# Moving the page gather of two of eight sequences from the second layer into the first, on one core

## What is computed

```python
# layer 0 (even): pooling and gating mixer, then a mixture of experts
y = concat([a_out, b_out]) @ w_out              # the first output projection
x = LN(alpha * x + y)
x = LN(alpha * x + moe(x))
# layer 1 (odd): RWKV-7 recurrence beside latent attention, then a mixture of experts
y = concat([y_c, y_d]) @ w_out
x = LN(alpha * x + y);  x = LN(alpha * x + moe(x))

# sample group, latent attention of layer 1: 2048 past positions = 16 pages of 128
def page_step(carry, pages):                    # scanned over page_table.T
    ck = pool_ckv[pages]                        # (8 sequences, 128 positions, 128)
    kp = pool_kpe[pages]                        # (8 sequences, 128 positions, 32)
    return online_update(carry, scores(q_lat, q_pe, ck, kp), ck)

# moe: 16 SwiGLU experts, 2 of them for each token
y += gates[:, e] * ((silu(h @ w_gate[e]) * (h @ w_up[e])) @ w_down[e])
```

## Time and profile before

| what | value |
|---|---|
| time, median of 3 runs | 1121.46 us (1120.9 to 1131.64) |
| span of the profiled execution | 1120.2 us |
| mean granted TensorE clock | 0.959 |
| TensorE matmul busy | 1026.5 us, 92% |
| TensorE weight load busy | 676.0 us, 60% |
| VectorE busy | 497.7 us, 44% |
| ScalarE busy | 330.4 us, 29% |
| GpSimd busy | 116.9 us, 10% |
| DMA | 225.32 MB, mean 201 GB/s |

### The profile page before, as it was taken

The page is one execution under the profiler, slowest core; times in us unless marked ns, Lnnn a source line. Parts: engine busy times, 40 slices in busy tenths (PEclk is TensorE's granted clock), DMA queues, the critical chain, the costliest instruction groups (busy, mean ns, idle before and its releaser), DMA issues.

```text
span 1120.2 us, 25522 instructions
## 1 busy us (share of the span) xinstructions
PE 1026.5 (92%) x10346; PEld 676.0 (60%) x10346; DVE 497.7 (44%) x1257; ACT 330.4 (29%) x877; POOL 116.9 (10%) x140
## 2 busy tenths in 40 slices
PE   9999997599998499999899999989999948999995
PEld 3687454466664267777788887656555535666641
DVE  1581134322222636497636653866623252222217
ACT  0102114133333233223334332165422132333321
POOL 0010000210000300000211110421000011100013
PEclk9999998699999699999999999899999978999998
DMA  9762204999996631122322233394353089999936
GB/s 317 298 88 65 109 38 194 334 351 373 371 402 251 218 151 60 54 86 75 95 75 77 73 115 99 110 388 183 127 222 150 19 324 285 375 372 378 413 105 222
DMA packets 80861, 225.32 MB, mean 201 GB/s; under 512 B 9424, under 2 KB 50432, under 8 KB 62432
## 3 DMA queue, kind: packets, MB, share of 16 engines
q1 hardware_dynamic: 65184, 153.29, 37.7%
q0 software_dynamic: 11968, 57.71, 15.6%
q10 hardware_dynamic: 3584, 12.58, 3.0%
HBM read 201.57 MB, written 40.86 MB: 216 GB/s over the span
## 4 chain that ended last, share of the span: by engine, by line
PE 86%; DMA 5%; DVE 4%; issue 4%; ACT 1%; POOL 0%; DVEq 0%; POOLq 0%; SPq 0%; ACTq 0%
PE bank L1352 16%; PE bank L1256 10%; PE bank L1543 9%; PE bank L1376 8%; PE bank L1451 6%; PE bank L1642 4%; PE bank L1477 3%; PE bank L1334 2%; PE bank L1514 2%; DMA xkept<-x 1%; PE bank L1896 1%; PE bank L1921 1%; PE bank L1267 1%; DMA work<-xkept,idx 1%; PE bank L1855 1%
## 5 line engine op out<-in xcount | busy, mean ns | idle before, releaser
L1256 PE MATMUL bank<-ring,cat 128*128 128x512 f32 x256 | 112.6, 594 | 1.3 <-ACT cat L2088 1.3
L1543 PE MATMUL bank<-xT,ring 128*128 128x288 f32 x448 | 110.9, 407 | 0.0
L1543 PEld LDWEIGHTS bank<-xT,ring 128*128 128x128 f32 x448 | 84.6, 190 | 23.8 <-issue 1.1
L1352 PE MATMUL bank<-ring,work 128*32 128x128 f32 (+1 forms) x1344 | 82.4, 317 | 1.7 <-DVE work L2537 1.7
L1256 PEld LDWEIGHTS bank<-ring,cat 128*128 128x128 f32 x256 | 47.5, 190 | 57.2 <-issue 57.2
L2547 DVE TENSOR_TENSOR work<-work,bank 128x192 f32<-128x192 f32 x32 | 11.3, 354 | 156.3 <-ACT work L2048 156.3
L2556 DVE COPY work<-bank 64x512 f32<-64x512 f32 x64 | 44.0, 688 | 67.2 <-PE bank L1376 66.7
L1352 PEld LDWEIGHTS bank<-ring,work 128*32 128x32 f32 (+1 forms) x1344 | 57.8, 121 | 24.7 <-issue 12.7
L1451 PE MATMUL bank<-xT,ring 128*128 128x288 f32 x256 | 63.1, 407 | 0.0
L2048 ACT ACTIVATE work<-bank 128x192 f32<-128x192 f32 x32 | 10.6, 331 | 162.3 <-PE bank L1352 162.3
L1451 PEld LDWEIGHTS bank<-xT,ring 128*128 128x128 f32 x256 | 48.3, 190 | 13.5 <-issue 0.4
(11 more groups left out here) (459 smaller groups left out, 1893.8 us busy)
## 6 DMA issues: line engine op xcount, KB each, us to landing
ring<-in_stream_dram SPq DMA_DIRECT2D x61, 1024.0 KB, 9.9
work<-in_stream_dram SPq DMA_DIRECT2D x16, 1024.0 KB, 17.1
cat<-in_stream_dram SPq DMA_DIRECT2D x16, 1024.0 KB, 19.1
by_batch<-in_pages_dram SPq DMA_DIRECT2D x128, 128.0 KB, 2.4
x<-in_stream_dram SPq DMA_DIRECT2D x12, 1024.0 KB, 18.3
xT<-in_stream_dram SPq DMA_DIRECT2D x12, 1024.0 KB, 17.3
yrows<-work ACTq DMA_DIRECT2D x32, 384.0 KB, 7.4
lnp<-in_ln_dram POOLq DMA_DIRECT2D x4, 1024.0 KB, 15.2
```

What stands on the lines that cost most here:

```text
L1256: i = pe.matmul(bank(n)[0:ROWS[tile], :], cat[:, k, tok(tile)], slot(w[k // 4], 4, 512)[:, k % 4, :], start=(k == 0), stop=(k == KC - 1))
L1352: i = pe.matmul(by_half[rows * q:rows * q + rows, :, to:to + width], xgT[:, e % 2, k, at:at + rows], w[:, :, width * q:width * q + width], ...
L1543: i = pe.matmul(bank(n + s)[:, 0:nn], slot(w, KC, 256)[:, k, P * (m % 2):P * (m % 2) + P], xT[:, k, a:a + nn], start=(k == 0), stop=(k == ...
```

## The change

SP gathers the pages of the first two sequences (`EARLY_BATCHES` = 2) in layer 0, in the branch that holds the spare loads of the expert stage, ahead of the wait for `0.o4` that stands there and ahead of the loads into `cat`. The other six stay where all eight were. Each of the moved pages issues the same two copies, of the same size. The page table is loaded by POOL with its first inputs, behind `even` and ahead of `buf`.

```diff
@@ in the program of SP
+            def bring_together(b):
+                for i in range(NPG):
+                    page = sp.value_load(table[0:1, b * NPG + i:b * NPG + i + 1], min_val=0, max_val=A["pages"].shape[0] - 1)
+                    sp.dma_start(by_batch[b, :, :, P * i:P * i + P],
+                                 A["pages"][bass.ds(page, 1), :, :].rearrange("o p (w n) -> (o p) w n", w=2))\
+                        .then_inc(batch_gathered[b], 16)
+                    g, at = i // 4, NPG * P + P * (i % 4)
+                    sp.dma_start(by_batch[b, D_ROPE * g:D_ROPE * g + D_ROPE, 0, at:at + P],
+                                 A["pages_kpe"][bass.ds(page, 1), :, :].rearrange("o r n -> (o r) n"))\
+                        .then_inc(batch_gathered[b], 16)
...
                 if key == ("scratch", 0):
 
-                    sp.wait_ge(table_loaded, 16)
-                    for b in range(DEC_B):
...
+                    for b in range(EARLY_BATCHES, DEC_B):
+                        bring_together(b)
...
                     layer = key[1]
                     rest = range(n, FIRST_EXPERT_BLOCK[layer] + 3 * N_EXP)
+                    if layer == 0:
+                        sp.wait_ge(table_loaded, 16)
+                        for b in range(EARLY_BATCHES):
+                            bring_together(b)
                     take(sp, job(f"{layer}.o{NT - 1}"))
                     for j in AHEAD[2:4]:
                         load_spare(layer, j)
@@ in the program of POOL
             pool.wait_ge(xT_loaded[NT - 1], 16)
             pool.dma_start(even, A["even"]).then_inc(even_loaded, 16)
+            pool.dma_start(table[:, :], A["table"]).then_inc(table_loaded, 16)
             pool.wait_ge(cleared, 1)
...
-            pool.dma_start(table[:, :], A["table"]).then_inc(table_loaded, 16)
             pool.wait_ge(ln_done, 2 * NT)
```

More of the change, by code:

```diff
@@ L320 @@
 NPGB = 3
+EARLY_BATCHES = 2
 PART = D_EXP // 2 + D_EXP // 4
```

## The result

| | median | runs |
|---|---|---|
| before, beside it | 1122.95 us | 4 (1120.9 to 1131.64) |
| changed kernel | 1159.14 us | 4 (1157.24 to 1161.61) |

The ratio is 1.031, 95% interval 1.027 to 1.036: 3.1% slower, about 35 us. The forecast was 1157, with a range of 1143 to 1170. The profiled execution has a span of 1155.4 us, 35.2 more than before.

What follows compares the result with a forecast made beforehand. TensorE, busy for 92% of the span, was taken as the bound. A 25 us stall at expert 2, growing to +36 us by expert 10, on 1120.2 gave 1156, and 1157 as median; range 1143 to 1170.

Steps and rivals of the forecast that it cites:

- Where the new code runs: In layer 0, SP reaches the early gather at about 184.6 us, behind the first output projection and not beside it.
- SP's time: Issuing the 32 early pages keeps SP from about 184.6 to 250 us, delaying every weight block from 7 on.
- The first stall: At expert 2 in layer 0, block 7 lands at 254.9 instead of in time for 229.67; TensorE stands for 25 us.
- No catching up: From expert 2 to 10, saturated DMA engines set the pace; expert 10 starts at 339.9, 36 us late.
- the correction for two sequences: In the 24 blocks before expert 10, fewer row gathers and stores with a slower TensorE take off 3.7 us.
- The pace after expert 10: TensorE sets the pace again, 45.6 us to expert 15 as before, and the 36 us delay stays to the end.
- The clock: The stall at expert 2 lowers TensorE's clock, 1.8 us there, with nothing added because block landings set the pace.
- I add nothing: The lowered clock at expert 2 adds 0 to the total, since the landings of the blocks are the limit.
- upper rival: In the expert stage, slower pages or clock lost at short waits cost +46 to +60 us; chance 0.10.
- Bandwidth: Weight blocks move at the trace's 420 GB/s; the skill's 358 GB/s limit would add up to 11 us.
- Layer 1: Its gather, 32 pages shorter, ends some 66 us earlier; nobody waits for it, so 0, 1 us either way.

Runs made afterwards that it cites:

- e1: The changed kernel with the 32 pages issued right behind the two loads into `work`, beside the output projection; 0.9988 of the kernel before.
- e3: The kernel before plus, in the place of the early gather, 32 page reads and 64 copies of 16 KB to an unused array; 1.0344 of the kernel before.
- e5: The changed kernel with the 32 pages behind the loads into `cat` and `x` instead of ahead of them; 1.0264 of the kernel before.
- e7: The changed kernel with three sequences gathered early instead of two; 1.0584 of the kernel before.
- e8: The changed kernel with 60 matmuls of unused result in front of TensorE's wait for block 7; 1.0504 of the kernel before.
- e2: The changed kernel with one sequence gathered early instead of two; 1.0129 of the kernel before.
- e9: The changed kernel with 30 matmuls of unused result in front of TensorE's wait for block 7; 1160.2 us, 1.0318 of the kernel before.
- e4: The kernel before plus, in the place of the early gather, six large copies of the same bytes to an unused array; 1.007 of the kernel before.

## Why the prediction was right

- *Where the new code runs.* SP reached it at 184.6 to 185.8, behind the projection. Right; e1 shows that the same code 73 us earlier in SP's time is free.
- *SP's time.* 62.8 to 71.9 us were allowed, 65.4 taken (to 250), 63.3 measured. e3 shows it is the cause: a fifth of the bytes, the same cost.
- *The first stall.* 25 us forecast, 27.3 measured. Block 7 was due at 254.9 and landed at 255.1. TensorE was ready 1.9 us sooner than before; 1.6 of them are that the rows of expert 0 landed in 5.2 us, not 6.8. The DMA share beside them was lower, 0.71 against 1.01 from 200 to 210 us, so it was likely the weights out of their way. The delay of expert 2 is 25.4 us.
- *No catching up.* Expert 10 was due at 339.9 and started at 338.39; 3.47 us a block against 3.54 (3.59 less 1.2/24). The forecast counted 8 gathers and 8 stores beside the 24 blocks, and 7 of each landed. e5 and e7 agree, and e8 shows that with enough lead there is no growth. e2 shows the weak place of this term: the price of a block depends on how many row gathers fall beside it, and I took the correction for two sequences over to one, where it doesn't hold. One sign was too broad: waits were expected before each of experts 4 to 10, and there are four of 0.7 us and more, before 5, 8, 9 and 10. Nor did the chain show 5 to 8% of DMA: it shows 4%, and books the waits as "issue".
- *The pace after expert 10.* TensorE alone, 45.6 us, was forecast. There was one more wait of 1.6 us, and it took 47.4. That the total still fits to half a us at expert 15 is luck: expert 10 was 1.5 us ahead of the forecast, and this wait was not in it.
- *The clock.* 1.8 us at expert 2 was forecast and 2.7 measured, and "I add nothing" holds (e9). Of the upper rival's clock losses at each short wait only one came: expert 5's group took 7.25 us behind a wait of 1.7. The waits before experts 8 to 11, 0.7 to 1.6 us, cost no clock. The Trainium skill ("TensorE: Matmul & The Clock Gate", Part 1) warns that waits for DMAs throttle TensorE again. The runs agree for the first stall and for some of the short waits (1.7 us in the changed kernel, 2.0 in e9), not for others (1.8 us in e2, 3.2 in e7).
- *Bandwidth.* Between 340 and 370 us the changed kernel moved 403 GB/s at a DMA share of 1.02. The 358 GB/s of the Trainium skill ("DMA: Bandwidth & Descriptors", Specifications) didn't bind this core.
- *Layer 1.* 0 with 1 us either way was forecast. Expert 15 is 36.5 late and the span 35.2, so 1.3 us came back in that one execution. They came back in the recurrence, which took 134.1 us against 135.7 from the first to the last matmul of L1642 (L1648 in the changed kernel), and the attention is as long as before. With e1 at 0.9988 (0.9971 to 1.0006) it isn't shown to be a gain.

## What to carry to other kernels

A queue that issues transfers in program order is a resource with its own time: moving cheap little copies to another place in it costs their issue time there, whoever moves the bytes, minus the time in which the queue would have waited anyway. Look for the place where the queue waits with nothing behind it that could run, not for the place where the engines look idle. And when the stage behind lives from a prefetched lead, as here, a stall is not paid once: as long as the transfers are saturated the lead doesn't come back.

## What the runs showed of the hardware that was not expected

- An issue can hold SP for long. Two loads of 1 MB take it 0.80 us at 110.97, and 0.98 us at 184.59, behind four blocks that are being moved. In e4 two copies of 1 MB from DRAM to DRAM in rows of 512 bytes took 11.37 us to issue, at nearly the same place behind the same four blocks. Which of the two, the rows or the direction, costs the time, no run separates.
- Each float32 matmul stands twice in the records (x60 for 30, x14 for 7), and a 128 x 512 one takes 0.86 us at the full clock (25.75 / 30).
- Executions differ by the clock in the recurrence of layer 1. The profiled execution of e3 took 8 us more there (144 us against 136), with one new wait of 2.1 us; that of e8 took 144 us too. The clock of e3 shows the rest; below it the stretch of the kernel before that answers to it:

```profile
704.50:734.50 30.00, 27.12 (x343) 20.93 (x340) 8.36 (x22) 9.08 (x24) 0.00 (x0) 0.77 0.40 128
```

```profile
670.00:700.00 30.00, 28.97 (x473) 22.57 (x473) 12.21 (x31) 9.20 (x23) 0.00 (x0) 0.99 0.39 121
```

In these two executions it explains most of what lies between expert 15 and the span: +33.6 and +43.4 us in e3, +49.8 and +60.4 in e8. The other executions of them have no trace. It is why a comparison at one point of the chain is sharper here than one of medians.
